# Recurrence heads 2 to 8: the first tap of the convolutions on ScalarE instead of VectorE, with edits at four borders of the kernel

## The chip, the cores and the metric

The kernel runs on one core of one Trainium2 chip. The metric is the device time of one execution in microseconds (us). A core has five engines, each with its own in-order instruction stream: TensorE (PE, matrix products), VectorE (DVE), ScalarE (ACT), GpSimd (POOL) and SyncE (SP, which issues most DMAs). They meet through semaphores.

## The reference, cut to what matters

Two blocks run one after the other on 512 tokens of width 1024, in fp32. The first has four mixers in a row, each with an RMS norm before it and a residual behind it:

```python
for i in range(DEPTH):                 # conv, fox, gdn, swa
    h = rms_norm(x, norm_w[i])
    y = ...                            # the mixer
    x = x + y
x = rms_norm(x, final_norm_w)
```

Conv is a gated short convolution, fox an attention with forget gates, gdn a gated delta rule, swa attention in a sliding window. The second block has three branches side by side (stick-breaking attention, an mLSTM, attention over a memory of 256 rows), gates over them and a feed-forward part. The change touches the first block alone, above all gdn. Per head of 128 it makes q, k and v by a causal convolution of four taps over the tokens, a silu and, for q and k, a unit norm, and then runs over the tokens in chunks of 64:

```python
qkv = silu(causal_conv(qkv, w_conv))   # y[t] = sum_k w[k] * u[t - 3 + k]
q, k = l2norm(q), l2norm(k)
T = solve(eye + L, eye)                # per chunk, L = strict((k*beta) k^T * decay)
u, w = T @ v_beta, T @ (k_beta * exp(g_cum))
v_new = u_c - w_c @ state              # from chunk to chunk
o = qd @ state + qk_c @ v_new
state = state * exp(g_last) + kd^T @ v_new
```

## The kernel before, in words

Activations lie transposed in the on-chip memory, as eight tiles of 128 channels x 512 tokens. A projection (`project`, L1835) is made with three matmuls for each 128-deep piece, w_hi x_hi, w_hi x_lo and w_lo x_hi (L1868 to L1870), where `hi` is a value rounded for the fast fp32 format and `lo` what rounding left. The very first three tiles go through `first_tile` (L1939), which needs x piece by piece as it comes.

Weights stream through the kernel in one fixed list of units of up to 512 KB. SyncE starts a unit's DMA into one of three raw buffers, GpSimd rounds it to `w_hi` (L406), VectorE subtracts `raw - w_hi` to get `w_lo` (`subtract`, L434, by the instruction at L424), and TensorE waits for that before the tile's first matmul. On VectorE the function `weights(t)` issues all subtractions up to the tile `t` and a little ahead, and most calls of it stand inside `take(t)`, ahead of the eviction of tile `t` from its PSUM bank (three banks take turns; `evac` multiplies by the norm factor `rstd`). All orders are written by hand: what stands later in VectorE's code runs later, whether or not its input was ready before.

The gdn mixer works head by head, r = 0 to 7 ("heads 2 to 8" are r = 1 to 7). While the recurrence of head r - 1 runs, `fill` on TensorE puts single pieces (three matmuls) of the projection of head r between its steps; generators `gdn_tile` on VectorE (L668) and ScalarE (L1448) are stepped beside it. A head has four projected tiles, the parts 0 (q), 1 (k), 2 (v) and 3 (the gate z). For parts 0 to 2 VectorE evicts the tile into `u`, makes the first tap with a tensor_scalar (`ts`, L427) into `t`, and adds three more taps with a scalar_tensor_tensor each (`stt`, L430); ScalarE applies silu and squares q and k; one part later TensorE sums these squares (`gdn_tile` on PE), ScalarE makes the factor (`root`, a Ln and an Exp, L1310), and VectorE scales q or k by it, behind the convolution of that later part. In the recurrence TensorE inverts the triangular matrix by levels; the last products of it are X6 and U6, and from then on each chunk needs v_new (a copy from PSUM on VectorE, L820) and the state (a copy, L827).

At the end of swa, eight tiles of output projection are added to x; for each, VectorE makes the normed x in two halves (`normed`: `xw_hi`, a tensor_scalar, and `xw_lo`, a scalar_tensor_tensor), subtracts weights, and adds up squares that ScalarE made (`add_both`), for the second block's norms.

## Time and profile before

| | |
|---|---|
| median of 3 runs | 2047.54 us (2047.34 to 2048.2) |
| profiled execution | 2048.57 us, its span 2046.7 us |
| TensorE busy | 2012.1 us (98%) |
| VectorE, ScalarE, GpSimd busy | 1465.6, 567.5, 348.9 us |
| mean granted TensorE clock | 0.997 of full speed |

A row of the timeline gives the start of an instruction (or of several like ones in a row) in us from the span's start, its length, engine, line and operation, its output and inputs by the program's names, and in brackets the idle time before it on its engine and what ended it. PE is TensorE, DVE VectorE, ACT ScalarE, POOL GpSimd. Matmul ends are modelled, so the distance from start to start tells a matmul's pace better than its length.

### The profile page before, as it was taken

Reading aid. Unit: us, or ns where it says so; the run is one execution under the profiler, and the core shown is the slowest. Engines: PE = TensorE matmul, PEld = TensorE weight load, DVE = VectorE, ACT = ScalarE, POOL = GpSimd, SP = SyncE. Lnnn points to the kernel's source line nnn. Section 1 sums busy time; section 2 is a strip of 40 time slices with the busy share of each in tenths; the row PEclk is TensorE's granted clock in tenths of the full one; section 3 lists DMA queues with packets and bytes.
Section 4 is the critical chain, followed back from the end, with each engine's and each line's share of the span. In section 5 each row is a group of like instructions: output and inputs, shape, how many; then the busy total and the mean of one; then the engine's idle time right before and its main releaser. Section 6 shows DMA issues by size and latency. Waiting matters only on the chain.

```text
span 2046.7 us, 32023 instructions
## 1 busy us (share of the span) xinstructions
PE 2012.1 (98%) x13030; PEld 1619.2 (79%) x13030; DVE 1465.6 (72%) x2288; ACT 567.5 (28%) x992; POOL 348.9 (17%) x317
## 2 busy tenths in 40 slices
PE   8999999999999999999999999999999999999999
PEld 6888788887777777778888877777888888888887
DVE  5766666667877777767998887576666778849973
ACT  2000122222454444423883233434310010000000
POOL 2211111111101011012111211111121212222221
PEclk9999999999999999989999999999999999999999
DMA  4323232222211121212222332111223332322232
GB/s 161 110 97 103 66 101 93 86 90 71 86 54 64 56 73 56 69 63 83 64 79 75 115 108 78 62 52 47 78 84 97 100 102 93 104 92 96 100 98 88
DMA packets 53362, 173.53 MB, mean 85 GB/s; under 512 B 6464, under 2 KB 6720, under 8 KB 53088
## 3 DMA queue, kind: packets, MB, share of 16 engines
q1 hardware_dynamic: 48112, 161.46, 23.8%
q10 hardware_dynamic: 5104, 10.03, 1.8%
q8 instruction: 104, 1.70, 0.3%
q14 instruction: 42, 0.34, 0.1%
HBM read 169.30 MB, written 2.16 MB: 84 GB/s over the span
## 4 chain that ended last, share of the span: by engine, by line
PE 89%; DVE 8%; issue 1%; ACT 1%; DMA 0%; DVEq 0%; SPq 0%; ACTq 0%
PE ps_lin L1868 24%; PE ps_lin L1870 23%; PE ps_lin L1869 23%; PE ps_att L1914 9%; PE ps_aux L1914 5%; DVE arena L424 2%; DVE arena L430 1%; PE ps_att L1923 1%; DVE w_lo L424 1%; ACT arena L1310 1%; PE ps_lin L1885 0%; DVE arena L427 0%; PE ps_lin L1887 0%; PE ps_lin L1886 0%; DVE xw_lo L430 0%
## 5 line engine op out<-in xcount | busy, mean ns | idle before, releaser
L1868 PE MATMUL ps_lin<-xw_hi,w_hi 128*128 128x512 f32 x1704 | 689.4, 405 | 3.8 <-DVE w_lo L424 3.7
L1870 PE MATMUL ps_lin<-xw_hi,w_lo 128*128 128x512 f32 x1704 | 665.6, 391 | 0.0
L1869 PE MATMUL ps_lin<-xw_lo,w_hi 128*128 128x512 f32 x1704 | 664.5, 390 | 0.0
L406 POOL TENSOR_SCALAR w_hi<-raw 128x1024 fp32r<-128x1024 f32 (+2 forms) x309 | 344.5, 1115 | 1680.3 <-PE ps_lin L1870 1556.1
L424 DVE TENSOR_TENSOR w_lo<-raw,w_hi 128x1024 fp32r<-128x1024 f32 (+2 forms) x341 | 379.9, 1117 | 45.6 <-POOL w_hi L406 17.0
L1310 ACT ACTIVATE arena<-arena 128x512 f32<-128x512 f32 (+7 forms) x331 | 206.4, 630 | 737.0 <-DVE arena L424 360.6
L1868 PEld LDWEIGHTS ps_lin<-xw_hi,w_hi 128*128 128x128 f32 x1704 | 320.3, 188 | 71.7 <-DVE w_lo L424 5.5
L1870 PEld LDWEIGHTS ps_lin<-xw_hi,w_lo 128*128 128x128 f32 x1704 | 319.9, 188 | 68.3
L1869 PEld LDWEIGHTS ps_lin<-xw_lo,w_hi 128*128 128x128 f32 x1704 | 320.8, 188 | 57.9
L424 DVE TENSOR_TENSOR arena<-ps_lin,rstd 128x512 f32<-128x512 f32 (+3 forms) x220 | 147.7, 671 | 197.5 <-PE ps_lin L1870 182.1
L1868 PE MATMUL ps_lin<-y_hi,w_hi 128*128 128x512 f32 (+1 forms) x544 | 206.0, 379 | 2.9 <-DVE w_lo L424 2.9
L1869 PE MATMUL ps_lin<-y_lo,w_hi 128*128 128x512 f32 (+1 forms) x544 | 205.7, 378 | 0.0
L1870 PE MATMUL ps_lin<-y_hi,w_lo 128*128 128x512 f32 (+1 forms) x544 | 205.7, 378 | 0.0
L430 DVE SCALAR_TENSOR_TENSOR arena<-arena,cols 128x512 f32<-128x512 f32 x206 | 155.7, 756 | 13.4 <-ACT arena L1310 6.2
L1914 PEld LDWEIGHTS ps_att<-arena 32*32 32x32 f32 (+3 forms) x1872 | 110.4, 140 | 43.7 <-issue 22.2
L1914 PE MATMUL ps_att<-arena 32*32 32x32 f32 (+8 forms) x1872 | 141.8, 250 | 2.7 <-ACT arena L1310 1.7
L1868 PEld LDWEIGHTS ps_lin<-y_hi,w_hi 128*128 128x128 f32 x544 | 103.2, 190 | 22.0 <-DVE w_lo L424 3.1
L1870 PEld LDWEIGHTS ps_lin<-y_hi,w_lo 128*128 128x128 f32 x544 | 103.1, 190 | 18.8
L1869 PEld LDWEIGHTS ps_lin<-y_lo,w_hi 128*128 128x128 f32 x544 | 103.1, 189 | 18.7
L424 DVE TENSOR_TENSOR x<-x,ps_lin 128x512 f32<-128x512 f32 x64 | 43.9, 686 | 92.1 <-PE ps_lin L1870 86.8
L424 DVE TENSOR_TENSOR arena<-arena 128x512 f32<-128x512 f32 (+5 forms) x124 | 86.5, 705 | 12.8 <-ACT arena L1310 9.2
L1316 ACT ACT_TABLE_LOAD x71 | 91.1, 1283 | 3.9 <-PEq L2473 1.7
(179 smaller groups left out, 1713.2 us busy)
## 6 DMA issues: line engine op xcount, KB each, us to landing
raw<-in_w_up SPq DMA_DIRECT2D x44, 512.0 KB, 3.2
raw<-in_conv_w_in SPq DMA_DIRECT2D x32, 512.0 KB, 3.2
raw<-in_fox_w_in SPq DMA_DIRECT2D x32, 512.0 KB, 3.2
raw<-in_gdn_w_in SPq DMA_DIRECT2D x32, 512.0 KB, 3.3
raw<-in_w_gate SPq DMA_DIRECT2D x24, 512.0 KB, 3.2
raw<-in_swa_w_in SPq DMA_DIRECT2D x20, 512.0 KB, 3.2
raw<-in_w_ml SPq DMA_DIRECT2D x16, 512.0 KB, 3.2
raw<-in_w_down SPq DMA_DIRECT2D x16, 512.0 KB, 3.5
```

Source lines behind the costliest of these rows:

```text
L406: pool.tensor_scalar(w_whole(n, kc * c)[0], w_raw(n, kc * c), 1.0, 0.0, mult, add).then_inc(s("w_rounded"), 1)
L424: return dve.tensor_tensor(o, p, q, op)
L430: return dve.scalar_tensor_tensor(o, p, sc, q, op0, op1)
L1310: return act.activation(o, i, func, **k)
L1316: act.preload_act_table_set(loaded[0])
L1868: pe.matmul(o, wh, hi, start=first and k == 0, stop=False)
L1869: pe.matmul(o, wh, lo, start=False, stop=False)
L1870: ins = pe.matmul(o, wl, hi, start=False, stop=last and k == kc - 1)
L1914: return pe.matmul(o, l, r, start=start, stop=stop)
L1923: return pe.transpose(o, i, mat("ident")[0:n, 0:n])
```

## The change

Five edits are made together. (1) TensorE runs 22 matmuls of 128x128 on a zeroed buffer before the first tile; nothing reads their result. (2) At fox's start VectorE subtracts the weights of the first tile before it waits for the norm factor, and those of the next before it waits for the softplus. (3) At gdn's start likewise the first tile's; the sums of squares of head 1 stand two and three pieces later on TensorE, and the scaling of its k comes before the convolution of its v. (4) In heads 2 to 8 the first tap is an activation with a column scale on ScalarE, for three parts each; VectorE waits for it before the second tap. (5) At the end of swa ScalarE makes `xw_hi`, and VectorE adds squares before it makes `xw_lo`. The order of GpSimd's and SyncE's instructions is the same as before.

The diff, cut:

```diff
         LAST_PIECE.update({LAST_FILL + at: (3 + i // BANKS, i % BANKS) for i, at in enumerate((1, 2, 4, 5, 7, 8))})
+        WARM = 22
+        FIRST_SQUARES = {2 * ND + 2: 1, 3 * ND + 1: 2}
         BRANCHES = ("w_sb_out_2", "w_ml_out_2", "w_xa_out_2")
...
                 w = mix_w[:, m:m + 1] if norm == 4 else col(name, base + m)
-                ts(xw_hi[:, m, :], x[:, m, :], w, mult).then_inc(s("x_ready"), 1)
+                if norm != 4:
+                    ts(xw_hi[:, m, :], x[:, m, :], w, mult).then_inc(s("x_ready"), 1)
                 dve.wait_ge(s("x_ready"), made("x_ready"))
...
+            weights(tile_of("fox_w_in", 0))
             dve.wait_ge(s("rstd_ready"), 2)
...
             ts(F["r1"][0:8, :], F["r1"][0:8, :], row("fox_b_f", 8), add).then_inc(s("softplus_in"), 1)
+            weights(tile_of("fox_w_in", FOX_H))
             dve.wait_ge(s("softplus_in"), made("softplus_in"))
...
             step(dve.memset(F["ones"][R8, :], 1.0))
+            weights(tile_of("gdn_w_in", 0))
             dve.wait_ge(s("rstd_ready"), 3)
...
                 evac(t, F["u"][:, 3:3 + T], ahead=False)
+                def scaled():
+                    dst = F["qkv"[part - 1]][:, r % 2, :]
+                    dve.wait_ge(s("gdn_rn"), 2 * r + part)
+                    stt(dst, dst, GDN_SCALE if part == 1 else 1.0, F["n"], mult, mult).then_inc(s("gdn_qk"), 1)
+                if part == 2 and r == 0:
+                    scaled()
                 yield
-                if n:
+                if n and r == 0:
                     dve.wait_ge(s("gdn_silu"), n)
-                step(ts(F["t"], F["u"][:, 3:3 + T], col("gdn_w_conv", 3 * 24 + j), mult))
+                if r == 0:
+                    step(ts(F["t"], F["u"][:, 3:3 + T], col("gdn_w_conv", 3 * 24 + j), mult))
                 for k in range(3):
                     yield
+                    if k == 0 and r:
+                        dve.wait_ge(s("gdn_tap"), n - 2)
                     if k == 1 and r == 0 and part == 2:
...
                 yield from weight_halves(t)
-                if part:
-                    dve.wait_ge(s("gdn_rn"), 2 * r + part)
-                    dst = F["qkv"[part - 1]][:, r % 2, :]
-                    stt(dst, dst, GDN_SCALE if part == 1 else 1.0, F["n"], mult, mult).then_inc(s("gdn_qk"), 1)
+                if part == 1 or part and r:
+                    scaled()
...
                     weights(tile_of("swa_w_out", 2 if m == 0 else 3))
+                if m:
+                    add_both(m - 1)
                 normed(m, 4)
...
                     weights(tile_of("w_mem_kv_2", 0))
-                if m == ND - 2:
-                    weights(tile_of("swa_w_out", ND - 1))
-                if m:
-                    add_both(m - 1)
             add_both(ND - 1)
...
                     return
+                def tap():
+                    t, n, j = tile_of("gdn_w_in", part * 8 + r), 3 * r + part, part * 8 + r
+                    act.wait_ge(bank_read(t), reads(t))
+                    activation(F["t"], F["u"][:, 3:3 + T], ACT.Copy, scale=col("gdn_w_conv", 3 * 24 + j)).then_inc(s("gdn_tap"), 1)
+                if r and part < 2:
+                    tap()
                 yield
...
                     root(F["n"], ps_aux[:], "gdn_rn")
-                for _ in range(4):
+                for i in range(4):
                     yield
+                    if i == 0 and r and part == 2:
+                        tap()
                 use(ACT.Silu)
...
                 act.wait_ge(bank_read(t), reads(t))
+                activation(xw_hi[:, m, :], x[:, m, :], ACT.Copy, scale=mix_w[:, m:m + 1]).then_inc(s("x_ready"), 1)
                 if m == 0:
...
             pe.wait_ge(s("mean_set"), 1)
+            for _ in range(WARM):
+                mm(ps_att[:, 0, 0:P], v_tmp[:, 0:P], v_tmp[:, 0:P])
...
                             project(1)
-                            if done[0] % ND == ND - 1:
+                            if r and done[0] % ND == ND - 1:
                                 gdn_tile(r, done[0] // ND)
+                            if r == 0 and done[0] in FIRST_SQUARES:
+                                gdn_tile(r, FIRST_SQUARES[done[0]])
                         if r == GDN_H and done[0] in LAST_PIECE:
```

VectorE in part 2 of head 3, beside the recurrence of head 2 (`u` is evicted in the first row, X6 in the row onto `spare`, `L820` and `L827` are the copies of v_new and of the state, `y_hi` and `y_lo` are the gated output of head 1), before:

```order
L424 TENSOR_TENSOR arena<-ps_lin,rstd 128x512 [waits unit_done,gdn_conv,gdn_T]
L427 TENSOR_SCALAR arena<-arena,cols 128x512 [waits gdn_silu,evacuated2]
L427 TENSOR_SCALAR spare<-ps_att 64x256 [waits gdn_XT,dve_step]
L430 SCALAR_TENSOR_TENSOR arena<-arena,cols 128x512 [waits gdn_X]
L430 SCALAR_TENSOR_TENSOR arena<-arena,cols 128x512 [waits dve_step] x2
L820 COPY arena<-ps_att 128x128 [waits gdn_vn]
L486 CAST y_hi<-v_tmp 128x512 [waits gdn_vn_out]
L424 TENSOR_TENSOR y_lo<-v_tmp,y_hi 128x512 [waits dve_step]
L827 COPY arena<-ps_aux 128x128 [waits gdn_S,y_ready]
```

The same place in the changed kernel:

```order
L426 TENSOR_TENSOR arena<-ps_lin,rstd 128x512 [waits unit_done,gdn_conv,gdn_T]
L429 TENSOR_SCALAR spare<-ps_att 64x256 [waits gdn_XT,evacuated2]
L432 SCALAR_TENSOR_TENSOR arena<-arena,cols 128x512 [waits gdn_tap,gdn_X]
L432 SCALAR_TENSOR_TENSOR arena<-arena,cols 128x512 [waits dve_step] x2
L836 COPY arena<-ps_att 128x128 [waits gdn_vn]
L488 CAST y_hi<-v_tmp 128x512 [waits gdn_vn_out]
L426 TENSOR_TENSOR y_lo<-v_tmp,y_hi 128x512 [waits dve_step]
L843 COPY arena<-ps_aux 128x128 [waits gdn_S,y_ready]
```

The tensor_scalar of the first tap is gone, and the first scalar_tensor_tensor has a wait for ScalarE's tap. ScalarE at this place, before (root's Ln and Exp, then the copies of U6 and of w):

```order
L1316 ACT_TABLE_LOAD
L1310 ACTIVATE arena<-ps_aux 128x512 [waits gdn_qk,gdn_ss]
L1310 ACTIVATE arena<-arena 128x512 [waits act_step]
L1310 ACTIVATE arena<-ps_att 64x4x64 [waits gdn_XU,gdn_rn]
L1310 ACTIVATE arena<-ps_att 128x512 [waits gdn_w]
```

And in the changed kernel:

```order
L1330 ACT_TABLE_LOAD
L1324 ACTIVATE arena<-ps_aux 128x512 [waits gdn_qk,gdn_ss]
L1324 ACTIVATE arena<-arena 128x512 [waits act_step]
L1324 ACTIVATE arena<-arena,cols 128x512 [waits evacuated2,gdn_rn]
L1324 ACTIVATE arena<-ps_att 64x4x64 [waits gdn_XU]
L1324 ACTIVATE arena<-ps_att 128x512 [waits gdn_w]
```

The tap stands between the root's Exp and the copy of U6; no table load is added for it. VectorE at the end of swa, the blocks of tiles 6 and 7, before:

```order
L424 TENSOR_TENSOR x<-x,ps_lin 128x512 [waits unit_done]
L427 TENSOR_SCALAR xw_hi<-x,mix_w 128x512 [waits evacuated1]
L430 SCALAR_TENSOR_TENSOR xw_lo<-x,mix_w,xw_hi 128x512 [waits x_ready]
L424 TENSOR_TENSOR w_lo<-raw,w_hi 128x1024 [waits w_rounded,xw_ready]
L424 TENSOR_TENSOR sq<-sq 128x512 [waits sq_ready]
L424 TENSOR_TENSOR arena<-arena 128x512 [waits sq_ready,sq_added]
L424 TENSOR_TENSOR x<-x,ps_lin 128x512 [waits unit_done,sq_added]
L427 TENSOR_SCALAR xw_hi<-x,mix_w 128x512 [waits evacuated2]
```

And in the changed kernel:

```order
L426 TENSOR_TENSOR x<-x,ps_lin 128x512 [waits unit_done]
L426 TENSOR_TENSOR sq<-sq 128x512 [waits sq_ready,evacuated1]
L426 TENSOR_TENSOR arena<-arena 128x512 [waits sq_ready,sq_added]
L432 SCALAR_TENSOR_TENSOR xw_lo<-x,mix_w,xw_hi 128x512 [waits x_ready,sq_added]
L426 TENSOR_TENSOR w_lo<-raw,w_hi 128x1024 [waits w_rounded,xw_ready]
L426 TENSOR_TENSOR x<-x,ps_lin 128x512 [waits unit_done]
L426 TENSOR_TENSOR sq<-sq 128x512 [waits sq_ready,evacuated2]
```

The tensor_scalar is gone from each block, the sums of squares stand ahead of `xw_lo`, and `xw_lo` waits for ScalarE's half.

## Rows read from the trace of the kernel before

**Rows 1.** The page, busy us (share of the span) x instructions.

```profile
PE 2012.1 (98%) x13030; PEld 1619.2 (79%) x13030; DVE 1465.6 (72%) x2288; ACT 567.5 (28%) x992; POOL 348.9 (17%) x317
```

**Rows 2.** Waits of PE: us in total, times, longest.

```profile
PE ps_lin L1944 <- DVE w_lo L424: 8.9, 1, 8.9
PE ps_lin L1868 <- DVE w_lo L424: 6.6, 4, 2.9
```

**Rows 3.** Windows: us; PE, PEld, DVE, ACT, POOL busy; PEclk, DMA share, GB/s.

```profile
860.00:900.00 40.00, 35.73 (x578) 28.45 (x578) 17.73 (x36) 13.67 (x29) 2.08 (x2) 0.87 0.16 53
1120.00:1140.00 20.00, 17.08 (x104) 15.38 (x103) 19.45 (x22) 3.73 (x7) 5.49 (x5) 0.91 0.32 109
```

**Rows 4.** Timeline of PE, the program's start: start, length, instruction, idle before.

```profile
9.46 0.63 PE L1945 MATMUL ps_lin<-xw_lo,w_hi 128*128 128x512 f32 x1
9.89 0.63 PE L1946 MATMUL ps_lin<-xw_hi,w_lo 128*128 128x512 f32 x1
...
15.34 0.40 PE L1944 MATMUL ps_lin<-xw_hi,w_hi 128*128 128x512 f32 x1
15.57 0.39 PE L1945 MATMUL ps_lin<-xw_lo,w_hi 128*128 128x512 f32 x1
```

**Rows 5.** Timelines of POOL and DVE, the program's start.

```profile
0.73 0.20 POOL L393 MEMSET v_tmp<- 128x128 f32 x1 [0.29 <-POOLq L2473]
...
11.79 1.22 DVE L424 TENSOR_TENSOR w_lo<-raw,w_hi 128x1024 fp32r<-128x1024 f32 x1
```

**Rows 6.** Timeline of PE, eight 128x128 fp32 products (16 records).

```profile
594.26 1.95 PE L1914 MATMUL ps_att<-arena 128*128 128x128 f32 x16
```

**Rows 7.** Timeline of DVE, the start of fox.

```profile
244.54 0.48 DVE L592 MEMSET arena<- 8x512 f32 x1 [3.57 <-ACT rstd L1310]
...
252.32 2.03 DVE L424 TENSOR_TENSOR w_lo<-raw,w_hi 128x1024 fp32r<-128x1024 f32 x1
```

**Rows 8.** Timeline of PE, the start of fox.

```profile
246.34 0.50 PE L1868 MATMUL ps_lin<-xw_hi,w_hi 128*128 128x512 f32 x1 [0.56 <-DVE w_lo L424]
...
254.41 0.50 PE L1868 MATMUL ps_lin<-xw_hi,w_hi 128*128 128x512 f32 x1 [2.33 <-DVE w_lo L424]
```

**Rows 9.** Timeline of PE, the start of gdn.

```profile
521.52 0.50 PE L1868 MATMUL ps_lin<-xw_hi,w_hi 128*128 128x512 f32 x1 [0.81 <-DVE w_lo L424]
...
528.41 1.13 PE L1914 MATMUL ps_aux<-sq,mats 128*128 128x384 f32 x4 [1.14 <-ACT sq L1310]
...
541.60 1.15 PE L1923 MATMUL ps_aux<-mats,arena 8*128 8x8 f32 x16 [0.23 <-DVE arena L424]
...
544.65 0.63 PE L1923 MATMUL ps_att<-mats,arena 128*128 128x128 f32 x4 [1.00 <-DVE arena L430]
```

**Rows 10.** Timeline of DVE, part 2 of head 3.

```profile
617.91 0.62 DVE L427 TENSOR_SCALAR arena<-arena,cols 128x512 f32<-128x512 f32 x1
...
619.78 2.33 DVE L430 SCALAR_TENSOR_TENSOR arena<-arena,cols 128x512 f32<-128x512 f32 x3
622.14 0.29 DVE L820 COPY arena<-ps_att 128x128 f32<-128x128 f32 x1
...
624.06 0.69 DVE L424 TENSOR_TENSOR w_lo<-raw,w_hi 128x512 fp32r<-128x512 f32 x1
625.03 0.29 DVE L820 COPY arena<-ps_att 128x128 f32<-128x128 f32 x1 [0.28 <-PE ps_att L1914]
```

**Rows 11.** Timeline of ACT: the root's Exp beside Rows 10; a scaled square.

```profile
619.30 0.63 ACT L1310 ACTIVATE arena<-arena 128x512 f32<-128x512 f32 x1
...
1113.57 0.71 ACT L1310 ACTIVATE arena<-x,cols 128x512 f32<-128x512 f32 x1
```

**Rows 12.** Timeline of PE, the recurrence of head 2 beside Rows 10.

```profile
623.24 0.38 PE L1914 MATMUL ps_aux<-arena 128*128 128x128 f32 x2
...
625.38 0.49 PE L1914 MATMUL ps_aux<-arena 128*128 128x128 f32 x2 [0.16 <-DVE arena L820]
```

**Rows 13.** Timeline of DVE, the end of swa.

```profile
1129.85 0.49 DVE L427 TENSOR_SCALAR xw_hi<-x,mix_w 128x512 fp32r<-128x512 f32 x1
```

## The prediction

> **What bounds the kernel now.** I read the page's busy shares first. TensorE is busy for 2012.1 of 2046.7 us [rows 1], so all its waits together are 34.6 us; whatever the change does must come out of these, or out of time in which TensorE works at the lower level of its clock. VectorE at 72% and ScalarE at 28% are off the bound as averages, and matter only where TensorE waits for them. So next I read TensorE's waits, which are few and named [rows 2]: 8.9 us once at the very start, and 6.6 us in four waits on VectorE's subtraction that makes w_lo. Third, the windows, for the clock that was granted in stretches with waits [rows 3]: 0.87 over 40 us at the end of the recurrence and 0.91 over 20 us at the end of the sliding-window mixer. Then the timelines of the places where the edits stand. The reader is to see that the four borders (program start, start of fox, start of gdn, end of swa) hold the long waits, while in heads 2 to 8, where most of the moved instructions are, TensorE hardly waits.
>
> The sum is made against the profiled execution: 2048.57 us, of which 2046.7 is its span and 1.9 lies outside. It is 1.03 us above the median of the runs, 2047.54.
>
> **Start (22 matmuls ahead of the first tile).** TensorE's first matmul starts at 8.9. Until about 14.4 its 512-column matmuls start 0.43 us apart (9.46 and 9.89), later 0.23 apart (15.34 and 15.57) [rows 4]: they begin at the lower of the two levels, 1.2 GHz, and go on at 2.4 GHz once TensorE has worked from 8.9 to 14.4. The change lets TensorE work from about 0.95, when the memset of v_tmp ends (0.73 + 0.20) [rows 5]. A 128x128 fp32 product costs 1.95/8 = 0.24 us at the upper level [rows 6] and so some 0.49 at the lower. If the level rises here as it did there, 11 products take 5.4 us and the other 11 some 2.7: they end at about 9.0, as the first real matmul becomes ready. That then runs at the upper level. Half of the stretch from 8.9 to 14.4 would be 2.75, but the second weight tile sets a limit: its w_lo is done at 11.79 + 1.22 = 13.0 on VectorE [rows 5], against 15.34 when TensorE starts that tile now [rows 4]. VectorE is not touched here, so the gain is 15.34 - 13.05 = 2.3. Bounds: 2.75 above; below, if the clock never rises for these small products, 22 x 0.49 = 10.8 ends at 11.7, a loss of 2.8 with the rest as slow as now. I take 2.3, since TensorE's clock rose on mere work here.
>
> **Start of fox (two subtractions moved).** VectorE stands idle for 3.57 us until ScalarE's norm factor comes [rows 7], and only then subtracts the weights of the first tile; TensorE waits 0.56 us for it and later 2.33 for the third tile's, which stands behind the softplus and the scan [rows 8]. Moved ahead, two subtractions of 1.22 [rows 5] fit into 3.57 (2.5); the third, 2.03 beside GpSimd's rounding [rows 7], goes into the softplus wait and ends near 250, four microseconds before it is needed. Gone: 0.56 + 2.33, and 0.11 for each restart (the first matmul after a wait takes 0.50, others 0.39): 3.1 us. Bounds 2.4 to 3.2: the first wait might stay. The next late thing is the tile after, whose subtraction now moves up too.
>
> **Start of gdn.** TensorE waits 0.81 for w_lo, 1.14 for ScalarE's squares, 0.23 for the columns and 1.00 for the scaled k [rows 9]: 3.18, with four restarts 3.6. The first goes as in fox. The squares are summed two or three pieces later (three matmuls of 0.23 each, so 1.4 or 2.1 us), so their wait goes. The scaling of k, moved ahead of the convolution of v, is done before TensorE wants it, and the 1.00 goes. But TensorE then reaches the columns 1.95 us earlier, while their input comes through ScalarE and the same VectorE queue, which moves up by about one subtraction (0.7): 1.95 - 0.7 = 1.25 us comes back as a longer wait there. Net 2.4. Bounds: 3.6 if the columns follow fully, 0.8 if they don't at all and the transposes still wait.
>
> **Heads 2 to 8 (21 first taps go from VectorE to ScalarE).** On VectorE 21 x 0.62 = 13.0 us disappear [rows 10], on ScalarE 21 copies with a column scale of 0.71 appear (the square with such a scale takes 0.71) [rows 11]. For parts 0 and 1 of a head both lie beside TensorE's own work, and I price them at nothing; TensorE's only waits in a head are about 0.16 for VectorE's copies [rows 12]. If this cover were gone, each tap would cost up to 0.71. Part 2 is different. There VectorE's tap (617.91 to 618.53) ran while VectorE had to wait anyway for the inverse's last product from TensorE, which the instruction between it and the next tap evicts: the next tap comes only at 619.78 [rows 10]. So nothing is saved. On ScalarE the tap comes behind the root, whose Exp ends at 619.30 + 0.63 = 619.93 [rows 11]: it ends near 620.7, and VectorE's three other taps, which began at 619.78, begin at 620.74. Behind them in VectorE's queue stand the copy of v_new, the cast and the y_lo of the gate, the state copy: 0.96 later each. The copy goes from 622.14 to 623.10, ends 623.39, and TensorE wanted it at 623.24 [rows 10, 12]: 0.2 lost. From there VectorE works nearly without a pause (cast, y_lo, state copy, half a subtraction) to 624.06 + 0.69 = 624.75, and then waits 0.28 for the second copy of v_new at 625.03 [rows 10]. 0.96 less that pause, rounded by the gap of 0.03, is 0.65: the second copy moves to 625.68 and TensorE's next step from 625.38 to 626.03 [rows 12], 0.65 lost per head, in which the 0.2 is contained. The first of the seven heads has no cast and no y_lo between the copies, so there only the 0.2 is lost. Sum 6 x 0.65 + 0.2 = 4.1 us lost. Bounds: 0 (later instructions have slack that I don't see) and 7 x 0.96 = 6.7.
>
> The rows say that the VectorE tap costs 0.62 and the ScalarE one 0.71, and that VectorE is busy for 1465.6 of 2046.7 us [rows 1]. The Trainium skill (Perfetto Trace Analysis, "Optimizing Scalar/DVE Operations") says that an operation which either engine can do is worth offloading to ScalarE when VectorE is saturated. In the heads VectorE waits at the tap's place, so by that rule this edit buys nothing; at the end of swa, with 19.45 of 20 us, the rule speaks for it, and the trace agrees. By the rule alone the head term would be 0 and the swa term the same.
>
> **End of swa (eight first halves go to ScalarE, order changed).** In 1120 to 1140 VectorE is busy for 19.45 of 20 us [rows 3], so it can't catch up there, and TensorE waits 2.9 us for its w_lo of the third memory tile, the longest of the four such waits [rows 2]. Each block loses a tensor_scalar of 0.49 [rows 13], with the gap behind it 0.52; eight blocks make 4.2 us, more than the 2.9 and a restart of 0.1. So the wait goes, and with it the stretch at the lower level behind it: (1 - 0.91) x 20 = 1.8 us. Gain 4.8. ScalarE pays 8 x 0.71 beside its 3.73 of 20. Bounds: 2.5 (part of the lag had other causes, and the clock falls as before) to 4.9. What is late next is the addition of the residual, still behind TensorE but off its path.
>
> **The last head** is not edited. It holds (1 - 0.87) x 40 = 5.2 us of lower clock [rows 3], and another phase of its waits may shift that by 2 us either way, which I take at 0.
>
> **Sum.** 2.3 + 3.1 + 2.4 + 4.8 - 4.1 = 8.5 us gained: 2048.57 - 8.5 = 2040.1 for a profiled execution, and 1.0 less, 2039.0, against the median.
>
> **Rivals.** *The head loss doesn't appear*: the copy has slack or GpSimd's rhythm lets VectorE catch up. For it speaks that VectorE loses 13.0 us of work in the heads, against it that the copy of v_new ended only 0.8 us before TensorE wanted it (622.43 and 623.24 [rows 10, 12]), less than the 0.96. Then 2039.0 - 4.1 = 2034.9. *The warm-up doesn't warm*: small products leave the clock low, and they delay the first tile. For it: no row shows such products at the lower level. Against it: the clock rose on the first tile's work, which pauses too. Time: without gain 2041.3, with the loss of 2.8 2044.1. *Half of the border gains are given back* because the next instruction is as late: gains 12.6 / 2 - 4.1 = 2.2, so 2045.3, no change that could be told. *Slower*: ScalarE's order becomes the bound in the heads. Its place is the three taps per head, each standing ahead of an exponential or a copy that TensorE needs; if each delays TensorE by its full 0.71 beside the 0.65 above, a head loses 2.8 us, seven lose 19.5, and the time is 2047.5 - 12.6 + 19.5 = 2054.4. It decides from 2.4 us a head on. Against it: ScalarE is busy for 567.5 us in all [rows 1], and its idle time is mostly beside the heads.
>
> **How the numbers follow.** A measurement of this kernel can tell 0.2% (4.1 us) from no change: faster is below 2043.4, slower above 2051.6. Chances: forecast 0.50 (own range 2036.5 to 2041.5), head loss absent 0.24, no warm-up 0.15 (a third of it above 2043.4), half given back 0.06, slower 0.05. That makes faster 0.50 + 0.24 + 0.10 = 0.84, within 0.2% 0.05 + 0.06 = 0.11, slower 0.05. The range goes from 2032.5 (head loss absent and the clock of the last head better by 2) to 2043.5 (warm-up with half its loss).
>
> **What would show it.** Start: TensorE's first real matmuls 0.23 apart, the second tile at about 13.0. Fox: no wait on w_lo between 244 and 255. Gdn: one wait of about 1.3 at the columns, none at the squares. Heads: a scaled copy right behind the root's Exp on ScalarE, VectorE's taps of part 2 starting with its end, and a TensorE wait for the copies of v_new grown to about 0.8 a head in six of the seven. Swa: the first matmul of the third memory tile without a wait, the clock at 1.00 in that window. The prediction is wrong if heads lengthen by more than 1 us each, or not at all, or if the first tile still runs at 0.43.

## The result and the profile after

The changed kernel takes 2037.65 us (median of 4 runs, 2037.21 to 2039.05), the kernel before beside it 2047.87 us (4 runs, 2047.34 to 2051.07). The ratio is 0.9946, 95% interval 0.9933 to 0.9958: faster by 0.5%, more than the 0.2% that a measurement can tell. 2039.0 was predicted, and the range held. The profiled execution took 2037.56 us with a span of 2035.8, 10.9 us less than before.

The page's busy shares of the changed kernel, as in [rows 1]:

```profile
PE 2015.5 (99%) x13074; PEld 1620.3 (80%) x13074; DVE 1447.7 (71%) x2258; ACT 587.8 (29%) x1021; POOL 347.8 (17%) x317
```

TensorE has 44 more records (22 products in two passes each). Its idle time went from 34.6 to 20.3 us. VectorE lost 30 instructions net (21 taps and 8 first halves among them) and ScalarE gained 29.

The waits of TensorE (us in total, times, longest), as in [rows 2]:

```profile
PE ps_aux L1940 <- DVE arena L836: 2.7, 16, 0.2
...
PE ps_aux L1949 <- DVE arena L426: 2.0, 1, 2.0
...
PE ps_att L1940 <- issue: 1.5, 2, 1.2
```

The wait of 8.9 at the first tile and the four for w_lo at L1868 are gone. In their place stand one wait of 2.0 for the columns of gdn and a stall of 1.2 that the profile can't explain by a semaphore ("issue"). The windows, as in [rows 3]:

```profile
860.00:900.00 40.00, 34.74 (x420) 27.96 (x409) 20.10 (x37) 12.98 (x27) 3.25 (x3) 0.91 0.15 50
1120.00:1140.00 20.00, 20.00 (x161) 19.26 (x160) 16.12 (x19) 4.85 (x8) 5.86 (x5) 1.00 0.40 134
```

At the end of swa TensorE is busy without a gap at the full clock, and VectorE has fallen from 19.45 to 16.12 of 20 us.

To see where the 10.9 us lie, each matmul of the trace before was set beside the same one after (they come in the same order but for two sums of squares), and the lead of the changed kernel was followed through the program:

| stretch | predicted | lead gained |
|---|---|---|
| start, until the fourth tile | 2.3 | 2.1 |
| start of fox | 3.1 | 3.5 |
| start of gdn, until the first head's recurrence | 2.4 | 2.5 |
| recurrence of heads 1 to 7 | -4.1 | -1.5 |
| last head | 0 | -0.4 |
| end of swa | 4.8 | 4.7 |
| elsewhere | 0 | 0.1 |
| sum, at the last matmul | 8.5 | 11.0 |

Four of the terms came out within 0.4 us. The heads did not: they lost 2.6 us less. Inside that row, by the same comparison: the two steps at the copies of v_new lose 0.37 us beside head 1 and 0.54 to 0.58 beside each of six more, 3.7 in all (predicted 0.2 and 0.65, 4.1). But 0.20 us is gained in each of six heads at a place that the prediction had priced at nothing, 1.2 in all, and another 0.52 just ahead of the recurrence, which the table counts with the start of gdn. The rest, about 1 us net, are stalls without a semaphore that stand elsewhere than before; since these come and go (below), that part of the smaller loss is luck.

The loss first. VectorE in part 2 of head 3 and ScalarE beside it, in the changed kernel, as in [rows 10, 11]:

```profile
611.90 0.43 DVE L429 TENSOR_SCALAR spare<-ps_att 64x256 f32<-64x256 f32 x1 [1.44 <-PE ps_att L1940]
613.37 2.33 DVE L432 SCALAR_TENSOR_TENSOR arena<-arena,cols 128x512 f32<-128x512 f32 x3 [1.04 <-ACT arena L1324]
615.73 0.29 DVE L836 COPY arena<-ps_att 128x128 f32<-128x128 f32 x1
```

```profile
611.88 0.63 ACT L1324 ACTIVATE arena<-arena 128x512 f32<-128x512 f32 x1
612.54 0.72 ACT L1324 ACTIVATE arena<-arena,cols 128x512 f32<-128x512 f32 x1
613.32 0.38 ACT L1324 ACTIVATE arena<-ps_att 64x256 f32<-64x256 f32 x1
```

The scaled copy comes right behind the root's Exp, takes 0.72, and VectorE waits 1.04 for it. The time that VectorE saves by not making the tap shows as a longer wait ahead (1.44). The three taps then start 1.0 later relative to TensorE than before. The prediction's sign for this, waits for the copies of v_new grown to 0.8 a head, is not in the list of waits: there they are 2.7 us in 16 waits, and before they were

```profile
PE ps_aux L1914 <- DVE arena L820: 2.5, 15, 0.2
```

The loss stands in the starts of TensorE's rows at the two copies, which don't hang on modelled ends. Before, and then in the changed kernel:

```profile
623.01 0.40 PE L1870 MATMUL ps_lin<-xw_hi,w_lo 128*128 128x512 f32 x1
```

```profile
615.59 0.40 PE L1896 MATMUL ps_lin<-xw_hi,w_lo 128*128 128x512 f32 x1
616.07 0.49 PE L1940 MATMUL ps_aux<-arena 128*128 128x128 f32 x2
...
618.52 0.49 PE L1940 MATMUL ps_aux<-arena 128*128 128x128 f32 x2 [0.16 <-DVE arena L836]
```

Before, the products behind the first copy began 0.23 after the row at 623.01, and those behind the second 2.14 later (623.24 and 625.38 [rows 12]); now it is 0.48 and 2.45, so 0.56 is lost in this head.

The gain: VectorE at the start of part 0 of a head, ahead of a level of the inverse, before and then after.

```profile
684.60 0.68 DVE L424 TENSOR_TENSOR arena<-ps_att,arena 128x512 f32<-128x512 f32 x1
685.20 0.48 DVE L427 TENSOR_SCALAR arena<-arena,cols 128x512 f32<-128x512 f32 x1
685.71 2.33 DVE L430 SCALAR_TENSOR_TENSOR arena<-arena,cols 128x512 f32<-128x512 f32 x3
687.96 0.28 DVE L424 TENSOR_TENSOR spare<-ps_att,mats 128x128 f32<-128x128 f32 x1
```

```profile
677.96 0.68 DVE L426 TENSOR_TENSOR arena<-ps_att,arena 128x512 f32<-128x512 f32 x1
678.56 2.32 DVE L432 SCALAR_TENSOR_TENSOR arena<-arena,cols 128x512 f32<-128x512 f32 x3
680.80 0.29 DVE L426 TENSOR_TENSOR spare<-ps_att,mats 128x128 f32<-128x128 f32 x1
```

Here nothing makes VectorE wait: it runs without a pause from the eviction to the masking of the level's product (onto `spare`), for which TensorE waited 0.2 us. Without the tap that comes 0.5 earlier in the row, and TensorE's wait is gone: its first product on `spare` began at 688.39, 0.52 behind the last product ahead of it, and begins now at 681.54, 0.31 behind it. Beside the first recurrence the same wait was longer, and it is gone too, before and then after:

```profile
557.68 0.74 PE L1914 MATMUL ps_att<-spare 32*32 32x32 f32 x64 [0.51 <-DVE spare L424]
```

```profile
549.63 0.74 PE L1940 MATMUL ps_att<-spare 32*32 32x32 f32 x64
```

In part 1 of the head above VectorE has to wait for TensorE at the masking two rows behind the tap. Without the tap only that wait grows, from 0.67 to 1.20 us, before and then after:

```profile
695.67 0.29 DVE L424 TENSOR_TENSOR spare<-ps_att,mats 128x128 f32<-128x128 f32 x1 [0.67 <-PE ps_att L1914]
```

```profile
688.84 0.29 DVE L426 TENSOR_TENSOR spare<-ps_att,mats 128x128 f32<-128x128 f32 x1 [1.20 <-PE ps_att L1940]
```

### The profile page after: what moved, and what is told of

Same layout as the page of the kernel before. It is cut to its first block, busy times and chain, and to the rows that moved or that the text cites. A ratio compares the mean times of both kernels' runs of the same rounds, so it can differ in the third digit from the quotient of the medians.

```text
span 2035.8 us, 32118 instructions
## 1 busy us (share of the span) xinstructions
PE 2015.5 (99%) x13074; PEld 1620.3 (80%) x13074; DVE 1447.7 (71%) x2258; ACT 587.8 (29%) x1021; POOL 347.8 (17%) x317
## 4 chain that ended last, share of the span: by engine, by line
PE 88%; DVE 8%; ACT 3%; issue 1%; DMA 0%; DVEq 0%; SPq 0%; ACTq 0%
PE ps_lin L1894 24%; PE ps_lin L1896 23%; PE ps_lin L1895 23%; PE ps_att L1940 8%; PE ps_aux L1940 4%; DVE arena L432 2%; ACT arena L1324 2%; DVE arena L426 2%; PE ps_att L1949 1%; DVE w_lo L426 1%; PE ps_lin L1911 1%; ACT L1330 0%; PE ps_lin L1913 0%; PE ps_lin L1912 0%; DVE arena L429 0%
```

## The experiments

Theory 1: the v tap (part 2) on ScalarE costs 3.7 us, the q tap (part 0) gains 1.2 and 0.5, the k tap does nothing. The main rival: the differences in the heads are another phase of the queues or of instruction fetches, or the relief of VectorE acts in more places than these.

**v tap back on VectorE.**

```diff
-                if n and r == 0:
+                if n and (r == 0 or part == 2):
                     dve.wait_ge(s("gdn_silu"), n)
-                if r == 0:
+                if r == 0 or part == 2:
                     step(ts(F["t"], F["u"][:, 3:3 + T], col("gdn_w_conv", 3 * 24 + j), mult))
...
-                    if k == 0 and r:
-                        dve.wait_ge(s("gdn_tap"), n - 2)
+                    if k == 0 and r and part < 2:
+                        dve.wait_ge(s("gdn_tap"), 2 * r + part - 1)
...
-                    if i == 0 and r and part == 2:
-                        tap()
```

> The changed kernel with the v part's first tap of heads 2 to 8 back on VectorE; the q and k taps stay on ScalarE. Theory 1 (the v tap on ScalarE ends 1 us after VectorE could go on, and the copies of v_new carry that to TensorE; in the trace of the changed kernel 0.33 us in head 1 and 0.56 to 0.59 in each of six more): 3.5 to 3.8 us faster than the changed kernel, about 2034, and TensorE reaches the first copy of v_new without a wait. Theory 2 (the loss at these copies comes from another phase of the queues, not from the tap): within 1 us of the changed kernel, 2037.7.

Measured: 2035.16 us (5 runs, 2033.93 to 2036.51), ratio to the kernel before 0.9930 (0.9917 to 0.9942). VectorE in part 2 of head 3:

```profile
612.06 0.62 DVE L429 TENSOR_SCALAR arena<-arena,cols 128x512 f32<-128x512 f32 x1
613.47 0.43 DVE L429 TENSOR_SCALAR spare<-ps_att 64x256 f32<-64x256 f32 x1 [0.79 <-PE ps_att L1938]
613.93 2.33 DVE L432 SCALAR_TENSOR_TENSOR arena<-arena,cols 128x512 f32<-128x512 f32 x3
```

The three taps follow the eviction at once again. Matched matmul by matmul, TensorE regains 0.37 us at the copies of v_new in the first head and 0.55 to 0.57 in each of the six others: 3.72, against 3.74 lost by the change. The median moved by only 2.5 because the profiled execution, and probably others, lost 1.6 us at the start of gdn in a stretch of lower clock that the changed kernel's trace hadn't. Theory 1 holds; theory 2 falls, since the loss at each copy came back with the tap and with nothing else on TensorE changed.

**All 21 taps back on VectorE**, the four borders as changed.

```diff
-                if r == 0:
+                if True:
                     step(ts(F["t"], F["u"][:, 3:3 + T], col("gdn_w_conv", 3 * 24 + j), mult))
...
-                    if k == 0 and r:
-                        dve.wait_ge(s("gdn_tap"), n - 2)
...
-                if r and part < 2:
-                    tap()
...
-                    if i == 0 and r and part == 2:
-                        tap()
```

> The changed kernel with all 21 first taps back on VectorE; the four border edits stay. Theory 1 (the v taps cost 3.7 us, the q taps give back 0.2 us in each of six heads because an inverse's level waits for VectorE there, the k taps do nothing): 2.5 us faster than the changed kernel, about 2035.2, and the wait of 0.2 at the inverse's level is there again. Theory 2 (the q and k taps relieve VectorE by 8.7 us in all, and TensorE gets more of it than that wait shows): slower than the changed kernel, 2038 or more.

Measured: 2037.51 us (2035.85 to 2039.41), ratio 0.9941 (0.9929 to 0.9954). Relative to the changed kernel's trace TensorE gains the same 3.71 us at the copies of v_new, loses 0.20 at each of the six inverse levels (1.2) and 0.52 ahead of the recurrence. So the edit of the heads costs 3.7 - 1.2 - 0.5 = 2.0 us by itself. The times of the two kernels can't be told apart (0.9941 and 0.9946): of the 1.7 us between the spans the scatter of the executions leaves nothing sure, and the 2.5 us that theory 1 expected are not in the medians. What is shown is shown by the steps, not by the medians. The q and k taps went back together here; that the gain is the q tap's alone is read from the rows of parts 0 and 1 above, and no run moves one without the other. (The relief that theory 2 speaks of is 6.8 us, not 8.7: the taps of q and k take 0.48 and 0.49 us each on VectorE.)

**The heads' edit alone**, on the kernel before.

```diff
-                step(ts(F["t"], F["u"][:, 3:3 + T], col("gdn_w_conv", 3 * 24 + j), mult))
+                if r == 0:
+                    step(ts(F["t"], F["u"][:, 3:3 + T], col("gdn_w_conv", 3 * 24 + j), mult))
...
+                    if k == 0 and r:
+                        dve.wait_ge(s("gdn_tap"), n - 2)
...
+                if r and part < 2:
+                    tap()
                 yield
...
+                    if i == 0 and r and part == 2:
+                        tap()
```

> The kernel before with the 21 taps on ScalarE and nothing else of the change. Theory 1 (the edit of the heads is a loss by itself, whatever the borders do): 2.5 us slower than before, about 2050. Theory 2 (the heads gain or lose nothing; the trace's differences there are another phase of instruction fetches): within 1 us of 2047.5.

Measured: 2050.12 us (11 runs), the kernel before 2048.44 beside it, ratio 1.0006 (0.9997 to 1.0014). In the trace the same steps: 3.81 us lost at the copies of v_new, 1.2 and 0.51 gained; the span is 1.6 us longer. The direction and the steps are those of theory 1; the size in the medians lies between the theories, and the interval takes in no change.

**No matmuls ahead of the first tile.**

```diff
-        WARM = 22
+        WARM = 0
```

> The changed kernel without the 22 matmuls ahead of the first tile. Theory 1 (they only raise TensorE's clock before the first tile): 2.4 us slower than the changed kernel, about 2040, the first tile's matmuls 0.43 apart again; nothing else differs, apart from waits of TensorE that end with no semaphore (0.25, 0.17, 0.29 and 0.35 us before, 0.30 and 1.19 after), which go back to their old places if they are fetches of TensorE's instructions, whose boundaries the 22 matmuls shift. Theory 2 (those waits belong to the place in the program): the wait of 1.19 us in the last head stays.

Measured: 2040.08 us (2039.67 to 2041.6), ratio 0.9956 (0.9942 to 0.9969). The first tile's matmuls stand 0.43 apart again. That the median is just 2.4 us above the changed kernel's is partly chance: in the traces the start loses 1.4 us, the start of gdn another 1.6 to a lower clock that the changed kernel's trace hadn't, and 1.4 come back at the stall in the last head. The stall of 1.19 us in the last head is gone, and one of 0.2 stands in another head. But these stalls moved as well with the v tap back, where TensorE's instructions were the same: there 0.3 and 0.4 us. So they belong neither to a place nor to the number of instructions ahead alone.

**With 11 and with 18 matmuls ahead.** The same line with 11 and 18.

> The changed kernel with 11 instead of 22 matmuls ahead of the first tile; in its trace the spacing of these fell from 0.49 to 0.24 at about 5.9 us, so 11 end near 6.4 and TensorE stands idle for 2.5 us before the first tile. Theory 1 (TensorE must work right up to the first tile to keep the level): the tile's first matmuls 0.43 apart, as slow as without any, 2040. Theory 2 (the level, once reached, holds over such a pause at least as often as it fell behind the 2 us wait of gdn's start): 0.23 apart, 2037.7.

> The changed kernel with 18 instead of 22 matmuls ahead of the first tile; they end near 7.5, 1.3 us before it. Both theories of the run with 11 expect the upper level here and 2037.7; if the first tile runs at 0.43, the count of 22 was needed.

Measured: 2041.35 and 2040.43 us (4 runs each), ratios 0.9961 (0.9946 to 0.9976) and 0.9955 (0.9938 to 0.9971). TensorE at the first tile, with 11, then with 18, then in the changed kernel with 22:

```profile
9.01 0.80 PE L1972 MATMUL ps_lin<-xw_hi,w_hi 128*128 128x512 f32 x1 [3.72 <-DVE w_lo L426]
9.60 0.63 PE L1973 MATMUL ps_lin<-xw_lo,w_hi 128*128 128x512 f32 x1
10.03 0.63 PE L1974 MATMUL ps_lin<-xw_hi,w_lo 128*128 128x512 f32 x1
```

```profile
8.92 0.50 PE L1972 MATMUL ps_lin<-xw_hi,w_hi 128*128 128x512 f32 x1 [0.79 <-DVE w_lo L426]
9.26 0.40 PE L1973 MATMUL ps_lin<-xw_lo,w_hi 128*128 128x512 f32 x1
9.50 0.40 PE L1974 MATMUL ps_lin<-xw_hi,w_lo 128*128 128x512 f32 x1
```

```profile
8.87 0.50 PE L1972 MATMUL ps_lin<-xw_hi,w_hi 128*128 128x512 f32 x1 [0.37 <-DVE w_lo L426]
9.21 0.39 PE L1973 MATMUL ps_lin<-xw_lo,w_hi 128*128 128x512 f32 x1
9.43 0.39 PE L1974 MATMUL ps_lin<-xw_hi,w_lo 128*128 128x512 f32 x1
```

With 11 the level had already risen (from start to start a product took 0.43 at first and 0.22 at the end), and after 3.7 us of standing still, where 2.5 was expected, the tile ran at 0.43 again. So theory 2 of that run falls; theory 1 holds, though not to the letter, since after 0.8 and 0.4 us of standing still the level held. The trace with 18 is as fast over the start as with 22; its longer time comes from the start of gdn, where it lost 3.1 us to a lower clock.

**The changed kernel once more.** No edit.

> The changed kernel once more, beside the others of this set. Theory 1 (the half-level stretch at the start of gdn, 3.4 us long, that two of the earlier runs had and the changed kernel's trace didn't, comes and goes from execution to execution behind the 2 us wait at the columns): the times of its executions scatter by 1.5 to 2 us, 2037 to 2039.5. Theory 2 (it depends on the code): all within 0.5 us of the first median 2037.65. Waits that end with no semaphore will stand elsewhere than 1.19 us in the last head if they hang on the moment of a fetch.

Measured: 2038.59 us (2037.17 to 2040.78), ratio 0.9951 (0.9938 to 0.9963). The windows at the start of gdn, in this execution and in the first profile of the same kernel:

```profile
533.00:538.00 5.00, 3.02 (x25) 2.37 (x24) 4.89 (x7) 2.95 (x5) 1.23 (x1) 0.91 0.52 176
538.00:541.00 3.00, 3.00 (x10) 2.44 (x9) 2.93 (x9) 1.63 (x3) 0.00 (x0) 0.57 0.52 166
```

```profile
533.00:538.00 5.00, 3.03 (x27) 2.50 (x26) 4.89 (x7) 2.96 (x5) 1.22 (x1) 1.00 0.63 171
538.00:541.00 3.00, 3.00 (x16) 2.46 (x16) 2.93 (x9) 1.62 (x3) 0.00 (x0) 1.00 0.58 195
```

The same code ran at the upper level in one execution and partly at the lower in the other, 1.6 us apart there. Theory 1 of this run holds, though its executions scatter by 3.6 us, more than the 1.5 to 2 expected. The stall in the last head, 1.19 us in the first profile, was another time not of that size: TensorE gained 0.9 us at that matmul. It hangs on the moment.

**End of swa: ScalarE's copies without the new order, and the new order without the copies.**

```diff
-                if m:
-                    add_both(m - 1)
                 normed(m, 4)
                 if m == ND - 1:
                     weights(tile_of("w_mem_kv_2", 0))
+                if m == ND - 2:
+                    weights(tile_of("swa_w_out", ND - 1))
+                if m:
+                    add_both(m - 1)
```

> The changed kernel, but at the end of swa VectorE's order is that of before (squares added behind the normed x, the last weight tile pulled ahead); ScalarE still makes the eight first halves. Theory 1 (VectorE's load is what counts: 8 x 0.52 us less are enough to catch up): no wait for w_lo near 1120 to 1130, within 0.5 us of the changed kernel. Theory 2 (the order counts: the squares' sums and the weight tile stood ahead of the w_lo that TensorE needs): the wait comes back in part, 1 to 2 us, and with a lower clock behind it the kernel is 2 to 4 us slower than the changed one.

```diff
-                if norm != 4:
+                if True:
                     ts(xw_hi[:, m, :], x[:, m, :], w, mult).then_inc(s("x_ready"), 1)
...
-                activation(xw_hi[:, m, :], x[:, m, :], ACT.Copy, scale=mix_w[:, m:m + 1]).then_inc(s("x_ready"), 1)
```

> The changed kernel, but VectorE makes the first halves at the end of swa itself, in the changed order. Theory 1 (load counts): a wait of 2 to 3 us for the third memory tile's w_lo, 4 to 5 us slower than the changed kernel with the clock's share. Theory 2 (order counts): no wait, within 0.5 us.

Measured: 2043.17 us, ratio 0.9970 (0.9960 to 0.9979), and 2043.97 us, ratio 0.9974 (0.9964 to 0.9983), 9 runs each. Each half alone loses about 5 us of the change's gain. In the traces, relative to the changed kernel, the end of swa loses 4.1 us with the copies alone (the wait and a lower clock behind it), 4.3 with the order alone (waits at two tiles). The waits of TensorE at that place, copies alone, then order alone:

```profile
PE ps_lin L1896 <- DVE w_lo L426: 2.3, 1, 2.3
```

```profile
PE ps_lin L1893 <- DVE w_lo L426: 3.8, 2, 2.3
```

Why the copies alone don't help: VectorE in two blocks of that kernel.

```profile
1113.20 0.75 DVE L432 SCALAR_TENSOR_TENSOR xw_lo<-x,mix_w,xw_hi 128x512 fp32r<-128x512 f32 x1 [0.86 <-ACT xw_hi L1326]
...
1118.85 0.75 DVE L432 SCALAR_TENSOR_TENSOR xw_lo<-x,mix_w,xw_hi 128x512 fp32r<-128x512 f32 x1 [0.86 <-ACT xw_hi L1326]
```

In place of a tensor_scalar of 0.49 stands a wait of 0.86 for ScalarE's copy, so a block is no shorter: 5.65 us between these two rows, where a block took 5.34 before. In the changed order the sums of squares fill that wait. VectorE then waits for TensorE instead: in the changed kernel the residual's addition of a block has

```profile
1118.19 0.69 DVE L426 TENSOR_TENSOR x<-x,ps_lin 128x512 f32<-128x512 f32 x1 [0.95 <-PE ps_lin L1896]
```

Without that wait VectorE's own work in a block is 4.5 us (5.44 from addition to addition, less 0.95). Not all of it is the moved work: in each of the four kernels one addition of squares in a block runs beside GpSimd's rounding and takes longer than its 0.69 us, 1.42 before and with the copies alone, 1.51 with the order alone, but 0.99 in the changed kernel. Before, and then changed:

```profile
1114.34 1.42 DVE L424 TENSOR_TENSOR sq<-sq 128x512 f32<-128x512 f32 x1
```

```profile
1113.47 0.99 DVE L426 TENSOR_TENSOR sq<-sq 128x512 f32<-128x512 f32 x1
```

Both theories fall in their pure form: neither load nor order is enough by itself, the two together are. What of the gain is the filled wait, what the shorter addition, and what the last weight tile, whose subtraction the new order no longer pulls ahead, no run separates. The Trainium skill (Perfetto Trace Analysis, "Optimizing Scalar/DVE Operations") says that with a saturated VectorE it may make sense to give ScalarE some of its work (the prediction has "is worth" for this "may"). Here VectorE was busy for 19.45 of 20 us [rows 3], and the copies alone took 0.6 of the 2.9 us away: the trace agrees only once the wait for the other engine has work in it.

**v tap back, and the columns of gdn later on TensorE.** The edit of the v tap as above, and:

```diff
-                fill(GDN_FILL["tok"] - 1)
+                if h == 0:
+                    fill(1)
+                    gdn_columns()
+                fill(GDN_FILL["tok"] - (1 if h else 2))
...
                     fill(4 * ND - 2)
-                    gdn_columns()
```

> The changed kernel with the v tap of heads 2 to 8 back on VectorE, and at the start of gdn TensorE's transposes of the columns behind k's transposes and one more piece. Theory 1 (v taps cost 3.7; the 1.97 us wait at the columns is only a matter of order): 5.5 us faster than the changed kernel, about 2032, and no half-level stretch at the start of gdn in any execution. Theory 2 (what is late is VectorE's copy of the columns, so the wait moves to the first product that needs them): as fast as with the v tap alone, about 2034 to 2035.

Measured: 2033.83 us (2032.49 to 2034.08), ratio 0.9925 (0.9912 to 0.9939): faster than the kernel before by 0.75%, and than the changed kernel beside it (2038.59). The wait of 1.97 is gone and no lower clock stands at the start of gdn. But of the 1.97 only 0.5 us stays there relative to the first trace of the changed kernel, since TensorE now meets what was hidden behind that wait:

```profile
534.10 0.50 PE L1892 MATMUL ps_lin<-xw_hi,w_hi 128*128 128x512 f32 x1 [0.54 <-DVE w_lo L426]
546.36 0.68 PE L1938 MATMUL ps_att<-mats,spare 64*64 64x64 f32 x16 [0.45 <-DVE spare L426]
549.39 0.74 PE L1938 MATMUL ps_att<-spare 32*32 32x32 f32 x64 [0.19 <-DVE spare L426]
```

So theory 1 is right on the clock and on the v tap, and too large by 1.4 us on the wait; the time came out nearer to theory 2.

## Why the prediction was right, and where its steps were not

**The bound** was read rightly: TensorE's idle time fell by 14.3 us, while its busy time rose by 3.4, in which the 22 products alone are 7.5. VectorE's 18 us less work counted only where TensorE waited.

**Start.** Right in mechanism and nearly in size: the first real matmuls stood 0.23 apart, the second tile began at 13.08 where about 13.0 was said, and the w_lo of that tile was the limit. The lead was 2.26 at that tile and 2.15 behind it, since the first matmul after the wait took 0.11 longer, which the term leaves out. A product cost 0.43 at the lower level and not 0.49, so the 22 ended at 8.5 and not 9.0. That they ended just ahead of the tile mattered: with 11 the level was lost again. The size is partly luck, because it hangs on when the level rises in the kernel without them: at about 14.2 us in the trace of before, at about 12.7 in the run without the 22, and against that one they gain 1.4.

**Fox.** Right: both waits went, 3.5 us for 3.1. VectorE's two early subtractions took 2.36 us in the wait for the norm factor, and the third stood in the softplus wait. No run takes these two edits back; the steps of the matched traces, 0.8 and 2.6 us, stand at the two waits. The changed kernel's rows:

```profile
238.87 2.36 DVE L426 TENSOR_TENSOR w_lo<-raw,w_hi 128x1024 fp32r<-128x1024 f32 x2
...
245.05 1.20 DVE L426 TENSOR_TENSOR w_lo<-raw,w_hi 128x1024 fp32r<-128x1024 f32 x1
```

**Gdn.** Right in sum, 2.5 for 2.4, by errors against each other: gdn's own edits gave 1.9, and the first head's q tap, an edit of the heads, gave 0.52 in the same stretch. The step that failed is "But TensorE then reaches the columns 1.95 us earlier", from which "1.25 us comes back". Counted from the start of gdn, TensorE came to the columns 2.48 us earlier and their input 0.74, so 1.74 came back; and it came on top of the 0.23 us of before, which the sum had counted as gone. The wait is 1.97. That the 0.7 for the input came out is chance. VectorE began the product that makes this input 1.58 earlier, but it took 1.51 us in place of 0.67: before, GpSimd's next rounding began only when it had ended (at 541.53), now it runs beside it (533.46 to 534.68). It is so in all twelve traces, but no run moves the rounding alone. The product before, and then the product and the wait in the changed kernel:

```profile
540.87 0.67 DVE L424 TENSOR_TENSOR arena<-arena 8x512 f32<-8x512 f32 x1
```

```profile
533.70 1.51 DVE L426 TENSOR_TENSOR arena<-arena 8x512 f32<-8x512 f32 x1
```

```profile
535.26 1.15 PE L1949 MATMUL ps_aux<-mats,arena 8*128 8x8 f32 x16 [1.97 <-DVE arena L426]
```

And the price of that wait was missed: in 7 of 9 traces that have it, a stretch at the lower level follows, which costs 1.6 or 3.1 us; in none of the 3 traces without it. The changed kernel's first profile was one of the two without. So the median holds some of that loss, and the prediction had nothing for it.

**Heads.** The step that failed is "For parts 0 and 1 of a head both lie beside TensorE's own work, and I price them at nothing". It was argued from the waits for the copies of v_new alone. TensorE also waited at a level of the inverse, 0.2 us a head, and VectorE's queue ahead of it ran without a pause, so that the q tap stood on the path: 1.7 us in all. "In the heads VectorE waits at the tap's place" holds for parts 1 and 2, and not for part 0. The k tap is the only one that did nothing. The v tap's term was right in mechanism and nearly in size: 3.7 for 4.1, shown by taking that tap back alone (3.72 regained). The loss per head was 0.56, not 0.65, since the rows behind the tap closed up a little more than their lengths say: the second copy began at 618.17, while the half subtraction ahead of it, by its row, ran until 618.26.

**Swa.** Right in size, 4.7 for 4.8, wrong in the reason. The step "eight blocks make 4.2 us, more than the 2.9 and a restart of 0.1. So the wait goes" counts the tensor_scalar as saved. The run with the copies alone shows that it isn't: VectorE waits 0.86 for the copy. The wait went only with the new order besides, in which the sums of squares fill this 0.86; the shorter addition beside GpSimd's rounding, 0.4 a block, was not in the sum.

**The rivals.** That the head loss doesn't appear was the second likeliest; the loss appeared in full, and a gain of another part hid nearly half of it, which, with the 1 us of stalls, is why the time fell between the two. The warm-up did warm. Of the gains little was given back at once: the wait at the columns, and the clock behind it. That ScalarE's order becomes the bound in the heads found nothing beside the loss that was forecast: 0.56 us a head, where it needed 2.4.

**Slips in the sums**, none of which decided anything: the ends of the range, from their own reasons, are 2032.9 and 2042.7, not 2032.5 and 2043.5; the lower bound of gdn is 3.6 - 1.95 - 1.00 = 0.65, not 0.8; and 0.62 us is the price of the v tap, while those of q and k took 0.48 and 0.49, so that 11.2 us left VectorE in the heads and not 13.0.

## What to carry to other kernels

An instruction moved to an idle engine saves time only if its latency there, with the handover, is covered on the engine that waits for it: look at what stands next in that engine's queue, and put other work between. Where a queue runs without a pause up to something that the bounding engine waits for, even half a microsecond less shows; where it pauses anyway, the move only adds the other engine's queue. Price each place of a repeated edit by itself, since here three copies of one edit came out as a gain, nothing and a loss.

## What the runs showed of the hardware that was not expected

TensorE's clock fell to its lower level behind single waits of about 2 us in some executions of the same code and not in others, which cost 1.6 or 3.1 us; after 0.4 and 0.8 us it held, after 3.7 us it was lost. Beside GpSimd's rounding a product on VectorE took 1.51 us in place of 0.67, and additions 0.99 to 1.51 in place of 0.69. Stalls of 0.2 to 1.2 us, with no semaphore behind them, stood among the smallest products (32 columns, 64 of them in 0.74 us), and changed place and size from run to run. In the traces of before and after, the 16 KB transfers on the queue of instructions are 4 to 7 us apart in these stretches and some 28 us apart elsewhere; that the stalls are fetches that come late fits this, but no run here took the fetches away, so it stays open.
